# Branch gates and projections in 512-column chunks, laid out by token, in a hybrid decoder block

## The reference

```python
h = rmsnorm(x, g_pre_mix[l])
proj = h @ w_in[l]                     # q, k, v, gates of three branches, and bg: 3 * 2048 gate columns
y_a = nsa_attention(...)               # (256, 1024)
y_b = retention(q_r, k_r, v_r) * jax.nn.silu(rg)   # (256, 1024)
y_c = memory_attention(...)            # (256, 1024)
bgate = jax.nn.sigmoid(bg.reshape(B, S, N_BRANCH, D))
merged = (bgate[:, :, 0] * (y_a @ w_br_nsa[l])
          + bgate[:, :, 1] * (y_b @ w_br_ret[l])
          + bgate[:, :, 2] * (y_c @ w_br_mem[l]))
x = x + rmsnorm(merged @ w_o[l], g_post_mix[l])
```

## Time and profile before

| | |
|---|---|
| time, median of 3 runs | 1780.84 us (1780.52 to 1784.01) |
| time of the profiled execution | 1781.96 us |
| its span | 1779.6 us |
| PE busy | 1732.5 us (97%) |
| PE weight loads busy | 1583.2 us (89%) |
| DVE busy | 1093.9 us (61%) |
| ACT busy | 816.2 us (46%) |
| POOL busy | 40.8 us (2%) |
| read from HBM | 321.71 MB, 183 GB/s over the span |

### The profile page before, as it was taken

How to read it: one execution, slowest core, us unless ns; L and a number is a source line. 1 busy time by engine, 2 the same in 40 slices (tenths; PEclk the granted TensorE clock), 3 DMA queues, 4 the chain that set the end, 5 groups by cost and what they waited for, 6 DMA issues and landing times.

```text
span 1779.6 us, 30244 instructions
## 1 busy us (share of the span) xinstructions
PE 1732.5 (97%) x11273; PEld 1583.2 (89%) x11273; DVE 1093.9 (61%) x1409; ACT 816.2 (46%) x1092; POOL 40.8 (2%) x47
## 2 busy tenths in 40 slices
PE   6999999999999999999999799999999999999997
PEld 6998999999899999999998688888888888888885
DVE  5644567666575454464475567676676676676666
ACT  5533345444433434334444455454454454454453
POOL 0000000000030000000000000000000000000000
PEclk9999999999999999999999999999999999999998
DMA  8755459535655566666557556666656666656653
GB/s 255 226 178 176 142 155 285 158 114 165 194 161 164 180 184 181 193 197 180 172 192 238 164 165 190 190 189 189 191 187 188 193 183 188 193 184 189 190 187 118
DMA packets 283005, 327.70 MB, mean 184 GB/s; under 512 B 12727, under 2 KB 241192, under 8 KB 282408
## 3 DMA queue, kind: packets, MB, share of 16 engines
q1 hardware_dynamic: 282920, 326.47, 60.1%
HBM read 321.71 MB, written 3.67 MB: 183 GB/s over the span
## 4 chain that ended last, share of the span: by engine, by line
PE 94%; DVE 2%; DMA 1%; issue 1%; ACT 1%; SPq 0%; POOL 0%; DVEq 0%; ACTq 0%; POOLq 0%
PE bank L1162 19%; PE bank L1125 11%; PE bank L1127 11%; PE bank L1126 11%; PE bank L1164 9%; PE bank L1151 8%; PE bank L1153 8%; PE bank L1152 8%; PE bank L1138 1%; PE bank L1139 1%; PE bank L1140 1%; DMA wraw<-in_w_in 1%; ACT whi L492 1%; DVE arena L1021 0%; DVE wlo L716 0%
## 5 line engine op out<-in xcount | busy, mean ns | idle before, releaser
L716 DVE TENSOR_TENSOR wlo<-wraw,whi 128x1024 fp32r<-128x1024 f32 x592 | 727.9, 1237 | 494.2 <-ACT whi L492 493.0
L492 ACT ACTIVATE whi<-wraw 128x1024 fp32r<-128x1024 f32 x592 | 625.5, 1060 | 767.9 <-PE bank L1127 347.8
L1162 PE MATMUL bank<-hx,whi 128*128 128x512 f32 x1408 | 496.8, 398 | 0.2 <-issue 0.2
L1164 PE MATMUL bank<-hx,wlo 128*128 128x256 f32 x1408 | 394.5, 280 | 0.0
L1125 PE MATMUL bank<-hx,whi 128*128 128x256 f32 x1280 | 366.5, 286 | 0.3 <-DVE hx L759 0.3
L1127 PE MATMUL bank<-hx,wlo 128*128 128x256 f32 x1280 | 362.4, 283 | 0.0
L1126 PE MATMUL bank<-hx,whi 128*128 128x256 f32 x1280 | 362.3, 283 | 0.0
L1162 PEld LDWEIGHTS bank<-hx,whi 128*128 128x128 f32 x1408 | 264.7, 188 | 65.6 <-issue 0.6
L1164 PEld LDWEIGHTS bank<-hx,wlo 128*128 128x128 f32 x1408 | 265.8, 189 | 0.4
L1125 PEld LDWEIGHTS bank<-hx,whi 128*128 128x128 f32 x1280 | 245.8, 192 | 1.6 <-DVE hx L759 0.7
L1126 PEld LDWEIGHTS bank<-hx,whi 128*128 128x128 f32 x1280 | 245.8, 192 | 0.3
(11 more groups left out here) (216 smaller groups left out, 1960.5 us busy)
## 6 DMA issues: line engine op xcount, KB each, us to landing
wraw<-in_w_in SPq DMA_DIRECT2D x200, 512.0 KB, 3.7
wraw<-in_w_up SPq DMA_DIRECT2D x176, 512.0 KB, 3.9
wraw<-in_w_down SPq DMA_DIRECT2D x88, 512.0 KB, 4.1
wraw<-in_w_mem_kv SPq DMA_DIRECT2D x32, 512.0 KB, 3.6
wraw<-in_w_o SPq DMA_DIRECT2D x32, 512.0 KB, 4.3
wraw<-in_w_br_mem SPq DMA_DIRECT2D x16, 512.0 KB, 3.6
wraw<-in_w_br_nsa SPq DMA_DIRECT2D x16, 512.0 KB, 3.6
wraw<-in_w_br_ret SPq DMA_DIRECT2D x16, 512.0 KB, 3.6
```

The costliest lines, as they stand in the source:

```text
L492: nc.scalar.activation(whi[:, c], wraw[:, c], ACT.Copy).then_inc(hi_done, 1)
L716: V.tensor_tensor(wlo[:, c], wraw[:, c], whi[:, c].bitcast(F32), ALU.subtract).then_inc(lo_done, 1)
L1162: T.matmul(o[:, :], whi[:, c, k, t * P:(t + 1) * P], hx[:, :, k0 + k, :], start=first and k == 0, stop=False, skip_group_check=True)
L1164: e = T.matmul(o[:, 0:S], wlo[:, c, k, t * P:(t + 1) * P], hx[:, 0, k0 + k, :], start=False, stop=last and k == CK - 1, skip_group_check=True)
```

## The change

- bg0 to bg2 and br0 to br2 use `chunk_w` instead of `chunk_t`: groups of 8 chunks (bg) and of 4 chunks (br), four groups in a phase, 2 k-tiles x 512 columns in a chunk. SP loads the chunks in that shape. The number of chunks is the same.
- Gates and merged sum lie by token now. ACT takes two tanh behind each bg group, DVE makes two products (and two adds) behind each br group.
- w_o still needs the merged sum with features on the partitions. PE transposes it in four parts of 8 tiles into banks 4 and 5 (`merged_transposes`): part i - 1 behind the third chunk of br2's group i, the last part behind the third chunk of w_o's first group. ACT and DVE split from those banks.
- Octets and groups alternate between the pairs (0, 1) and (2, 7). A phase's first group waits only for its own pair, other than in mv and rg.
- The transposes of a retention row come behind the first chunk of the next quad, ahead of the next row's inner product, instead of behind the fourth chunk of their own quad; the inner product doesn't wait for `evac[1]`.
- Some loops of ACT, DVE and PE are written out.

The diff, cut (the same `PAIRS` also replace the bank numbers in mv, rg and w_o; `chunk_w` gets the pair instead of the first bank):

```diff
-NSA_LINKS, RET_LINKS = 11, 6
+NSA_LINKS = 11
+PAIRS = ((0, 1), (2, 7))
+DOWN_PAIRS = ((2, 3), (4, 5))
+NEW_PAIRS = ("mv", "rg")
 NSA_BEFORE, NSA_AFTER = (0, 1, 2), (3,)
...
             for n, (b, w) in enumerate(((2, w_br_mem), (0, w_br_nsa), (1, w_br_ret))):
-                loop(Q0[f"bg{n}"], 4, 2, cols(w_in, C_BG + b * D))
+                loop(Q0[f"bg{n}"], 4, 2, wide_cols(w_in, C_BG + b * D), into_wide)
                 if n == 1:
                     sp.wait_ge(r_d, RH)
                     sp.dma_start(GP, g_post_mix.to_broadcast([P, D])).then_inc(s_gpost, 16)
-                def pairs(i):
-                    at = [sp.snap(4 * GW * i + GW * j) for j in range(4)]
-                    return [lambda c, j=j: rows(w, 4 * (c % 2), at[2 * j + c // 2]) for j in range(2)]
-                loop(Q0[f"br{n}"], 2, 2, pairs)
+                def branch(i):
+                    at = [sp.snap(4 * GW * i + 2 * GW * j) for j in range(2)]
+                    return [lambda c, o=o: rows(w, 2 * c, o, 2 * GW, 2) for o in at]
+                loop(Q0[f"br{n}"], 2, 2, branch, into_wide)
             for j in range(2):
                 quad(Q0["wo"] + j, lambda c: rows(w_o, 8 * j + 2 * c, 0, 2 * GW, 2), lambda c: wide(wraw, c))
...
                 ahead(q + 1, (3,))
+            def gate_tanh(n, i):
+                act.wait_ge(pe_done, 4 * (Q0[f"bg{n}"] + 2 * i + 1) + 4)
+                for t in range(TT):
+                    e = nc.scalar.activation(token_rows(A_GATE, t, i), ps[PAIRS[i % 2][t]][:, :], ACT.Tanh, scale=0.5)
+                e.then_inc(evac[i % 2], 1)
+            def merged_hi(g):
+                for b in range(2):
+                    act.wait_ge(s_mt, 2 * g + b + 1)
+                    nc.scalar.activation(m_hi[:, 4 * g + 2 * b:4 * g + 2 * b + 2, :].rearrange("p k s -> p (k s)"), ps[4 + b][:, :],
+                                         ACT.Copy, scale=0.5).then_inc(s_mgh, 1)
             for n in range(3):
...
-                q0 = Q0[f"bg{n}"]
                 for b in range(2):
                     act.wait_ge(evac[b], G0[f"bg{n}"] // 2)
-                if n == 0:
-                    with act.Fori(0, 2) as i:
-                        for j in range(2):
-                            r, q = 2 * i + j, 2 * i + (q0 + j)
-                            ahead(q)
+                for i in range(4):
+                    q = Q0[f"bg{n}"] + 2 * i
+                    for j in range(2):
+                        ahead(q + j, (0, 1, 2))
+                        if j:
+                            gate_tanh(n, i)
+                        ahead(q + j, (3,))
+                        if n == 0 and i < 2:
+                            r = 2 * i + j
                             act.wait_ge(r_t, r + 1)
-                            nc.scalar.activation(r_hi[:, bass.ds(512 * r, 512)], ps[6][:, :], ACT.Copy).then_inc(r_h, 1)
-                            nc.scalar.activation(arena[:, bass.ds(1024 * i + (A_GATE + 512 * j), 512)], ps[j][:, :],
-                                                 ACT.Tanh, scale=0.5).then_inc(evac[j], 1)
-                with act.Fori(0, 2 if n == 0 else 4) as i:
-                    for j in range(2):
-                        k = 8 - (4 if n == 0 else 8) + j
-                        ahead(2 * i + (q0 + k))
-                        nc.scalar.activation(arena[:, bass.ds(1024 * i + (A_GATE + 512 * k), 512)], ps[j][:, :],
-                                             ACT.Tanh, scale=0.5).then_inc(evac[j], 1)
+                            nc.scalar.activation(r_hi[:, 512 * r:512 * (r + 1)], ps[6][:, :], ACT.Copy).then_inc(r_h, 1)
                 if n < 2:
                     plain(Q0[f"br{n}"], 2)
-            with act.Fori(0, 2) as i:
-                for j in range(2):
-                    for b in range(2):
-                        ahead(2 * i + (Q0["br2"] + j), (2 * b, 2 * b + 1))
-                        k = 4 * i + (2 * j + b)
-                        act.wait_ge(s_mg, k + 1)
-                        nc.scalar.activation(m_hi[:, bass.ds(2 * k, 2), :].rearrange("p k s -> p (k s)"),
-                                             arena[:, bass.ds(512 * k + A_MERGED, 512)], ACT.Copy, scale=0.5).then_inc(s_mgh, 1)
+            for i in range(4):
+                ahead(Q0["br2"] + i, (0, 1, 2))
+                if i:
+                    merged_hi(i - 1)
+                ahead(Q0["br2"] + i, (3,))
             act.wait_ge(s_var, 1)
             for i in range(4):
                 q = Q0["wo"] + 2 * i
-                ahead(q)
+                ahead(q, (0, 1, 2))
+                if i == 0:
+                    merged_hi(3)
+                ahead(q, (3,))
                 ahead(q + 1, (0, 1, 2))
                 act.wait_ge(pe_done, 4 * (q + 1) + 4)
                 for t in range(TT):
-                    nc.scalar.activation(work[:, 512 * t:512 * (t + 1)], ps[2 * (i % 2) + t][:, :], ACT.Square,
+                    nc.scalar.activation(work[:, 512 * t:512 * (t + 1)], ps[PAIRS[i % 2][t]][:, :], ACT.Square,
                                          accum_out=sq[:, 0, t, i:i + 1]).then_inc(s_sq, 1)
                 ahead(q + 1, (3,))
...
@@ -956,56 +970,59 @@
                     dve.wait_ge(r_h, r + 1)
                     V.tensor_tensor(r_lo[:, bass.ds(512 * r, 512)], ps[6][:, :], r_hi[:, bass.ds(512 * r, 512)].bitcast(F32),
                                     ALU.subtract).then_inc(r_l, 1)
-                ch.leave(2, RET_LINKS * 2)
+            def merged_lo(g):
+                for b in range(2):
+                    dve.wait_ge(s_mgh, 2 * g + b + 1)
+                    tiles = slice(4 * g + 2 * b, 4 * g + 2 * b + 2)
+                    V.scalar_tensor_tensor(m_lo[:, tiles, :].rearrange("p k s -> p (k s)"), ps[4 + b][:, :], 0.5,
+                                           m_hi[:, tiles, :].rearrange("p k s -> p (k s)").bitcast(F32),
+                                           ALU.mult, ALU.subtract).then_inc(s_mgl, 1)
             for n in range(3):
-                q0 = Q0[f"bg{n}"] + (4 if n == 0 else 0)
                 with dve.Fori(0, 2 if n == 0 else 4) as i:
                     for j in range(2):
-                        ahead(2 * i + (q0 + j))
+                        ahead(2 * i + (Q0[f"bg{n}"] + (4 if n == 0 else 0) + j))
                 for b in range(2):
                     dve.wait_ge(evac[b], G0[f"br{n}"] // 2)
-                with dve.Fori(0, 2) as i:
-                    ch.enter(i, (0, 8, 4)[n])
-                    for j in range(2):
-                        for b in range(2):
-                            q, k = 2 * i + (Q0[f"br{n}"] + j), 4 * i + (2 * j + b)
-                            gate, sum_ = arena[:, bass.ds(512 * k + A_GATE, 512)], arena[:, bass.ds(512 * k + A_MERGED, 512)]
-                            if n == 0:
-                                ahead(q, (2 * b, 2 * b + 1))
-                                dve.wait_ge(pe_done, 4 * q + (2 * b + 2))
-                                V.scalar_tensor_tensor(sum_, gate, 1.0, ps[b][:, :], ALU.add, ALU.mult).then_inc(evac[b], 1)
-                                continue
-                            tmp = work[:, W_TMP + 512 * b:W_TMP + 512 * (b + 1)]
-                            dve.wait_ge(pe_done, 4 * q + (2 * b + 2))
-                            ch.link(V.scalar_tensor_tensor(tmp, gate, 1.0, ps[b][:, :], ALU.add, ALU.mult))
-                            dve.sem_inc(evac[b], 1)
-                            e = V.tensor_tensor(sum_, sum_, tmp, ALU.add)
-                            if n == 1:
+                for i in range(4):
+                    q = Q0[f"br{n}"] + i
+                    ahead(q, (0, 1))
+                    if n == 2 and i:
+                        merged_lo(i - 1)
+                    ahead(q, (2,))
+                    dve.wait_ge(pe_done, 4 * q + 4)
+                    for t in range(TT):
+                        dst = work[:, W_TMP + 512 * t:W_TMP + 512 * (t + 1)] if n else token_rows(A_MERGED, t, i)
+                        ch.add(V.scalar_tensor_tensor(dst, token_rows(A_GATE, t, i), 1.0, ps[PAIRS[i % 2][t]][:, :], ALU.add, ALU.mult))
+                    ch.wait()
+                    dve.sem_inc(evac[i % 2], 1)
+                    if n:
+                        for t in range(TT):
+                            e = V.tensor_tensor(token_rows(A_MERGED, t, i), token_rows(A_MERGED, t, i),
+                                                work[:, W_TMP + 512 * t:W_TMP + 512 * (t + 1)], ALU.add)
+                            if n == 2:
+                                e.then_inc(s_mg, 1)
+                            else:
                                 ch.add(e)
-                                ahead(q, (2 * b, 2 * b + 1))
-                                continue
-                            e.then_inc(s_mg, 1)
-                            ahead(q, (2 * b, 2 * b + 1))
-                            dve.wait_ge(s_mgh, k + 1)
```

(82 more changed lines are left out.)

64 lines of the change are left out of this document (36 added, 28 removed).

## The result

| | before | after |
|---|---|---|
| median, on one chip | 1781.74 us (1780.52 to 1784.01, 4 runs) | 1762.32 us (1762.15 to 1763.32, 4 runs) |
| ratio, 95% interval | | 0.989 (0.9879 to 0.9902) |
| profiled execution, span | 1779.6 us | 1760.4 us |
| PE busy, matmuls | 1732.5 us | 1712.3 us, 9577 |

What follows compares the result with a forecast made beforehand. PE was taken to bound the kernel, at 94% of the span. The terms -22.6 + 3.4 - 1.1 + 0.8 + 1.4 sum to -18.1 us, from 1780.84 to 1762.7 us; 8-in-10 range 1759.5 to 1770.

Steps and rivals of the forecast that it cites:

- narrow to wide: bg0 to bg2 and br0 to br2: 144 chunks at 2.723 instead of 2.880 us, 22.6 us less on PE.
- merged transposes: br2 and wo's first group: PE transposes 8 merged tiles in each of four groups, 3.4 us more.
- gap before wo: Between br2 and wo: the first group waits only for its own, earlier emptied pair, 1.1 us less.
- retention rows: bg0: PE waits longer before the second product as transposes delay ACT's split, net 0.8 us more.
- stall behind X: wo's 9th chunk: w_o's transfer queued behind the X reload lands late, PE stalls 1.4 us.
- Rival C: bg and br phases: the wide form saves nothing, cost goes with the columns; 1785.3 us, chance 0.02.
- Rival D: br2: DVE becomes the bound, needing over 4 us more per group, so PE's time isn't saved; chance 0.01.
- the cover in br2: br2: DVE's split of slot 3 ends 5.3 us into the next group, PE wants it at 8.2: 2.9 us spare.
- rival A: X reload, retention rows and transposes cost their bounds of 4.1, 4.6 and 4.6 us: 1770.4 us, chance 0.20.
- Rival B: wo and bg0: X lands in time and the retention wait is covered; 1760.5 us, chance 0.13.
- the second estimate of X's landing: wo: w_o's transfer behind X lands 9.0 + 1.3 = 10.3 us after X's issue, at W + 21.7 (W: wo's start).

Runs made afterwards that it cites:

- the best version: Changed kernel with x reloaded after w_o's first four quads, ACT splitting before its row copy, POOL's rotation after the decays: 1759.02 us, then 1757.88 us.

## Why the prediction was right, point by point

| term | predicted | measured | from |
|---|---|---|---|
| narrow to wide | -22.6 | -23.0 | 144 x (2.880 - 2.720) |
| merged transposes | +3.4 | +3.6 | 4 x 0.90 |
| gap before wo | -1.1 | -1.2 | 47.25 - 46.08 |
| retention rows | +0.8 | +0.8 | -4.35 + 32 x 0.160 |
| stall behind X | +1.4 | +1.2 | 101.53 - 100.37 |
| sum | -18.1 | -18.7 | the whole stretch, -18.66 (before rounding) |

The retention term is what is left of its part of the ledger once the cadence is taken out; the others have a measurement each.

**The total.** The forecast of 1762.7 us and the measured median of 1762.32 lie closer than the terms do, and that is luck. The 18.1 us were taken from 1780.84 us, the median of three runs; on the chip that ran both kernels before had 1781.74, and the medians differ by 19.4 us. The stretch gave 0.6 us more than forecast.

**The cadence.** wo's window held the right size of a chunk, 2.723 against 2.720, and the theory under it, some 13 ns with each matmul beside its columns, was tested by itself: halved matmuls in an otherwise unchanged kernel gave 92.16 us. By the formula that the Trainium skill gives for an isolated gap (TensorE: Matmul & The Clock Gate, "Back-to-back issue gap") two halves would cost 2.5 ns more than one whole, an estimate; the traces of this stream don't agree with it, 240.0 ns against 226.7. Rival C falls with that.

**The gap before wo** was sized right, but the forecast saw too little in it. It priced the wait where the kernel before had a gap, and not what the wide form would have cost at the other changes of phase under a wait for both pairs: 15 us in all in the one profile of it, 13 of them gaps. The sum came out right because that cost never arose. Rival D and the cover in br2 held: no wait of PE on DVE or ACT in br2 in any profile but that of both pairs, whose gaps are at its changes of phase.

**The retention rows.** The sum was right, its pieces less so, and their misses cancel, which is luck. Against the 2.83 us that an unhindered chunk behind an inner product takes, the waits were 1.05, 0.64, 0.63 and 0.19 us. The forecast listed 0.9, 0.8, 0.8 and 0.4, while its sum had booked only 0.1 more than before for row 0, so 0.7. Before, the waits were 0.61 us in each of rows 0 to 2 and none in row 3. So they grew by 0.7 us in all where the sum had 1.0, and the 0.2 us expected from one interruption in place of two didn't show (0.1 more, not 0.2 less).

In row 1 the chain went as forecast (T is again the end of the quad's first chunk, 513.22): POOL's piece began 1.50 us behind T and ended at T + 2.80, and DVE's split ended 1.08 later, at T + 3.88. DVE pays only for the part of POOL's piece that is still to run, hence 1.67 us and not the 2.15 of before. Only the two ends were off. PE's second product began at T + 4.47 and not 4.6, and PE would have been ready at T + 3.84 and not 3.78. Row 0 was underrated, with 0.44 us more instead of 0.1. POOL came in the middle of DVE's split of slot 3, waited for it (1.71 us) and then held up the split of slot 0 (2.31). What is new against the kernel before is that DVE left rg's gate 0.14 us behind T and no longer 0.20 ahead of it: bg0's first chunk took 2.73 us and not 3.07.

The rule that the prediction cited for it, of the Trainium skill (SBUF — State Buffer, "Who interferes with whom"), bore out from both sides: DVE first, and POOL pays (1.23 and 2.22); POOL out of the way, and both take their own time (1.27, and 2.36 for two splits). I had not seen that the later place of the transposes is worth nothing now and 2.4 us once POOL is moved.

**The X reload** went by its steps: issue at 11.3 us into wo (11.4), landing at 21.4 (21.3 to 21.7), PE's 9th chunk at 23.85 (23.8 to 24.2). From start to start PE would have begun that chunk at 22.68 (forecast 22.65), so the stall of 1.17 us is the lower end of the 1.2 to 1.5 forecast, of which 1.4 was taken. That the landing is no constant shows in the halved version: 9.3 us, and twice the stall. The 10.2 us of before, on which rival A's bound of 4.1 rests, were not reached. Rival B, X in time and no more wait in the retention rows than before, falls with the 1.2 and the 0.7 us seen at these places.

**In the bounds.** Two numbers of the forecast's bounds don't hold as written, and nothing came of it. The 1.14 us for a group's transposes at their dearest should be 1.04 + 0.07 = 1.11 (4.4 us, not 4.6), and the 1.3 us that stands behind the 9.0 in the second estimate of X's landing is in no row.

What stays open lies outside the stretch: 0.5 us of the 19.2 between the spans, and about 2 us between the medians of the best version and of after on one chip. In the profiles, the clock around 305 us goes with about 1 us of each, ahead of the stretch. Why the clock falls there in some executions only, and what moves the part behind the stretch, no run here shows.

## What to carry to other kernels

Where PE is the bound, count its instructions at a given number of columns: the distance of starts in a steady window, for two forms side by side, gives the price of one more matmul (13.3 ns here, 23 us in all). Before widening a group's result to two banks, ask what the next group waits for: emptying then lies behind the last matmul, and only a wait for the banks that it really needs hides it. Look at a split that is longer than its twin for a GpSimd instruction beside it, and change which of the two comes first, before any work is moved on PE.

## What the runs showed of the hardware

- A fp32r matmul with its own weight load takes 120.0 ns at 256 moving columns and 226.7 at 512, at the full clock: 2.880 and 2.720 us a chunk in bg1 of the two kernels, 2.880 again in the halved version. The 256 columns more cost 106.7 ns, one column a cycle at 2.4 GHz; 13.3 ns stay in both widths.
- A DVE split with two SBUF inputs beside GpSimd pays only for the rest of the GpSimd instruction: 1.23 us alone, 1.67 when it came 0.7 us behind the start of a 1.3 us piece, 2.15 when it came 0.2 behind it. The other way round a GpSimd piece of 1.27 took 2.22.
- Eight transposes of 128 x 128 fp32 take 0.79 us start to start between fp32r chunks and 0.90 by the length of the phase; sixteen cost 0.87 more.
- A 512 KB transfer behind 2 MB on the same queue landed 7.9 us after its issue in after, 9.3 in the halved version, and 10.2 in the kernel before.
- The granted clock can stand at 0.50 after PE has waited: for 3.4 us around 305 us in 6 of 14 profiles (behind single waits of 1.2 to 1.7 us; the other eight have such waits too, at 1.00), for 6.8 us once, from the end of the 2.9 us gap of the version with both pairs.
